# Low-rank maps of an RWKV time mix on two column halves, and their second maps on row halves

## The chip, the cores and the metric

One Trainium2 chip, one of its cores. The metric is the device time of one execution in microseconds (us). A core has five engines that run on their own and meet through semaphores: TensorE (PE in the profile, with its weight loads as PEld), VectorE (DVE), ScalarE (ACT), GpSimd (POOL), and SyncE (SP), which here only issues DMA transfers. ACTq, SPq and so on are the sequencers of the engines, where DMA transfers are issued. Each engine runs its instructions in the order of its own program; a wait holds up everything behind it on that engine.

## The reference

The model is one long chain on 512 tokens of width 1024: a block with an RWKV-7 time mix and a feed-forward, a block with sparse attention and a feed-forward, and a second model's block. Everything is float32. The change touches only the inputs of the time mix (`_rwkv7_time_mix`), which come near the start:

```python
xx = h_prev - h
xs = h[None] + xx[None] * mu[:, None, None, :]
r, k, v = jnp.einsum('pbtd,pde->pbte', xs[:3], w_rkv)
xv, xw, xa, xg = xs[2], xs[3], xs[4], xs[5]
w = -jax.nn.softplus(-(w0 + jnp.tanh(xw @ w1) @ w2)) - 0.5   # decay, w1 is 1024x64, w2 64x1024
a = jax.nn.sigmoid(a0 + (xa @ a1) @ a2)                       # rate,  a1 is 1024x64, a2 64x1024
g = jax.nn.sigmoid(xg @ g1) @ g2                              # gate,  g1 is 1024x160, g2 160x1024
...
kk = kk / jnp.maximum(jnp.sqrt(jnp.sum(kk * kk, -1, keepdims=True)), 1e-12)
decay = jnp.exp(-jnp.exp(heads(w)))
_, y = lax.scan(_rwkv7_step, S0, (tm(rh), tm(decay), tm(kh), tm(vh), tm(-kk), tm(kk * ah)))
```

There are 16 heads of 64. The scan is computed in chunks of 64 tokens, two heads (128 features) at a time.

## The kernel before

Features lie on the 128 partitions, tokens along the free side; the width 1024 is KT = 8 tiles of 128, HD is 64, P is 128. PSUM has eight banks, `ps[:, b, :]`, each 128 partitions by 512 numbers. `mm` (L191) is one float32 product out = left^T right; the profile shows each as two passes on PE, each with its own weight load, so eight matmuls are sixteen rows.

`modulation` (to 36 us) reduces 16 tiles of weights on DVE as they arrive. `time_mix_inputs` follows:

- ACT makes `h` (the profile's branch_in) tile by tile, L299; POOL makes the token shift `xx`, L315; DVE mixes, `mix` L318: for each tile j the three low-rank inputs w, a, g into `tmp` (mixed_low_rank), which has two buffers a kind, so tile j waits for PE's `lora{j-2}`; after the eight tiles it mixes r, k and v, eight tiles each.
- PE, for each tile j, makes four products that accumulate over j: w (64 columns of weights, bank 0, partitions 0 to 63), a (64 columns, bank 1, partitions 0 to 63), g0 (128 columns, bank 2) and g1 (32 columns, bank 3). Before w, a and g0 it waits for the mix that it reads.
- After the last tile ACT reads the four banks: tanh of w, copy of a, sigmoid of g0 and g1 (L302 to L306).
- SP loads the constants of the recurrence (`cr`, const_recurrence) once `lora7` is done; this load brings the semaphore `once_in` to 32.

`recurrence` works on eight pairs of heads. PE first waits for the pair's weights, for ACT's `g1` and for `once_in` at 32. Then come the inputs of pair 0: the projections r into bank 1 and k into bank 0 (eight products each), `decay_and_rate(0)`: the second maps w2 and a2 for this pair, each with 64 rows of contraction, into banks 1 and 0, where ACT has by then read r and k; `kk_sum`, the projection v into bank 4, and `by_tokens`. Then eight turns, one a pair (`turn`). Turn i has five rounds k = 1 to 5, in each a product Y{k}, ACT's copy of it (L585), and from that X{k} and XT{k}. Between these the inputs of pair i+1 are made: r after round 1, k around round 3, `decay_and_rate(i+1)` between Y4 and the wait for ACT's copy of Y4, `kk_sum` after XT4, v around round 5. `each_head` (L433) makes a product for each of the two heads, on partitions 0 to 63 and 64 to 127.

On ACT, `k_input` copies k (L540), waits for DVE's kk0 and squares it (L542); in round 4 it copies Y4, then takes the sigmoid of the decay (L548) and of the rate (L550). The order of all this is written out by hand; nothing plans it.

Elsewhere in the kernel (L1547, L1591) the attention makes two heads' products beside each other: the logits with 64 rows of contraction for each head in a bank of its own, the sums over values with 64 columns for each head on the two partition halves.

Of the kernel before, what the change touches and what calls it, by code (L numbers as in the profile page):

```python
# [8 lines left out]
P = 128  # L9
T = 512  # L10
D = 1024
KT = D // P
# [4 lines left out]
HD = 64  # L17
# [13 lines left out]
ACT = mybir.ActivationFunctionType  # L31
# [70 lines left out]
def build(nc, d):  # L102

    ctx = ExitStack()
    with ctx:
# [33 lines left out]
        ps = ctx.enter_context(nc.psum_tensor("psum", [P, 8, T], F32))  # L139
# [44 lines left out]
        def wtile(s, k, rows=P, width=P, at=0):  # L184
            return slot[s][0:rows, at + k * width:at + (k + 1) * width]
# [5 lines left out]
        def mm(out, lhsT, rhs, start=True, stop=True):  # L191
            return nc.tensor.matmul(out, lhsT, rhs, start=start, stop=stop)  # L192
# [17 lines left out]
        once_in = sem("loaded_once")  # L210
# [62 lines left out]
        MIX = ["r", "k", "v", "w", "a", "g"]  # L273

        def time_mix_inputs(scope, hin, mods_ready):
# [18 lines left out]
            def act(act):  # L294
                act_done.enter(act)
                act.wait_ge(x_in, 16)
                act.wait_ge(*mods_ready)
                for j in range(KT):
                    nc.scalar.activation(h[:, j, :], x[:, j, :], ACT.Identity, bias=mod(0, SH1, j),  # L299
                                                    scale=mod(0, SC1, j)).then_inc(*act_done.step(f"hin{j}"))  # L300
                act.wait_ge(*pe_done(f"lora{KT - 1}"))
                nc.scalar.activation(lora["w"][0:64, :], ps[0:64, 0, :], ACT.Tanh).then_inc(*act_done.step("w"))  # L302
                nc.scalar.activation(lora["a"][0:64, :], ps[0:64, 1, :], ACT.Copy).then_inc(*act_done.step("a"))
                nc.scalar.activation(lora["g0"][:, :], ps[:, 2, :], ACT.Sigmoid).then_inc(*act_done.step("g0"))
                act.wait_ge(zeroed, 1)
                nc.scalar.activation(lora["g1"][0:32, :], ps[0:32, 3, :], ACT.Sigmoid).then_inc(*act_done.step("g1"))  # L306

            def pool(pool):
                pool_done.enter(pool)
# [25 lines left out]
            def pe(pe):  # L335
                pe_done.enter(pe)
                pe.wait_ge(once_in, 16)
                for j in range(KT):
                    w = first[:, j * 288:(j + 1) * 288]
                    for n, (bank, a, b) in enumerate([(0, 0, 64), (1, 64, 128), (2, 128, 256), (3, 256, 288)]):  # L340
                        m = min(n, 2)
                        if n < 3:
                            pe.wait_ge(*dve_done(f"{MIX[3 + m]}{j}"))
                        last = mm(ps[0:b - a, bank, :], w[:, a:b], tmp[:, m, j % 2, :], j == 0, j == KT - 1)
                    last.then_inc(*pe_done.step(f"lora{j}"))

            phase(sp=sp, act=act, pe=pe, dve=dve, pool=pool)
# [13 lines left out]
        def recurrence(scope, h, xs, lora, mix_pe, mix_act, mix_dve):  # L361
# [427 lines left out]
            def pe(pe):  # L789
# [13 lines left out]

                def decay_and_rate(p):
                    pe.wait_ge(*in_act("r", p))
                    mm(ps[:, 1, :], wtile(0, 24, HD), lora["w"][0:HD, :]).then_inc(*in_pe.step("w"))
                    pe.wait_ge(*in_act("k", p))
                    mm(ps[:, 0, :], wtile(0, 25, HD), lora["a"][0:HD, :]).then_inc(*in_pe.step("a"))

                def kk_sum(p):  # L810
                    pe.wait_ge(*in_act("kk sq", p))
# [139 lines left out]
                        last = each_head(bank(4)[:, c, :], yn[:, c, :], eye)  # L951
                    last.then_inc(*pe_done.step("y fm"))
                pe.wait_ge(*loads.arrived(0))
                pe.wait_ge(*mix_act("g1"))
                pe.wait_ge(once_in, 32)
                projection("r", 1, range(KT), True)
                projection("k", 0, range(KT), True)
                decay_and_rate(0)
                kk_sum(0)
                projection("v", 4, range(KT), True)  # L960
                by_tokens(0)
                for i in range(N):
                    turn(i, i < N - 1)
# [1910 lines left out]
```

## Time and profile before

| | us |
|---|---|
| median of 3 runs | 3135.13 (3133.73 to 3135.48) |
| the profiled execution's own time | 3136.09 |
| its span in the trace | 3134.3 |
| PE busy | 2868.2 (92%) |
| PE's weight loads busy | 2086.7 (67%) |
| DVE busy | 1424.7 (45%) |
| ACT busy | 1032.7 (33%) |
| POOL busy | 229.3 (7%) |

The profile has a page (busy times, the span in 40 slices, the chain of work that ended last, the costliest groups) and views of the trace that can be asked for a stretch of time. In the timeline each row has a start, a duration, engine, line, operation, "out<-in", the shape (for PE: rows of contraction * columns of weights, then the moving operand's partitions x elements) and xN, the number of instructions merged in the row; behind it stands how long the engine had been idle and what ended that. Numbers of a merged row are from the first start to the last end. In the windows view PEclk is the clock that PE was granted, 1.00 being 2.4 GHz and 0.50 being 1.2 GHz.

### The profile page before, as it was taken

Reading aid. Unit: us, or ns where it says so; the run is one execution under the profiler, and the core shown is the slowest. Engines: PE = TensorE matmul, PEld = TensorE weight load, DVE = VectorE, ACT = ScalarE, POOL = GpSimd, SP = SyncE. Lnnn points to the kernel's source line nnn. Section 1 sums busy time; section 2 is a strip of 40 time slices with the busy share of each in tenths; the row PEclk is TensorE's granted clock in tenths of the full one; section 3 lists DMA queues with packets and bytes.
Section 4 is the critical chain, followed back from the end, with each engine's and each line's share of the span. In section 5 each row is a group of like instructions: output and inputs, shape, how many; then the busy total and the mean of one; then the engine's idle time right before and its main releaser. Section 6 shows DMA issues by size and latency. Waiting matters only on the chain.

```text
span 3134.3 us, 47831 instructions
## 1 busy us (share of the span) xinstructions
PE 2868.2 (92%) x19030; PEld 2086.7 (67%) x19030; DVE 1424.7 (45%) x2257; ACT 1032.7 (33%) x1526; POOL 229.3 (7%) x220
## 2 busy tenths in 40 slices
PE   4998989888999989998999969999989898899998
PEld 1566666645888844565888848888565565688875
DVE  6466565534333226655333243333234676533335
ACT  1232332204432122544432144431011374344214
POOL 1122232201000010311000000000000100000000
PEclk9999999988999989999999989999869999999999
DMA  5222232232222201112222202322111001222212
GB/s 191 85 99 92 102 119 92 89 114 81 94 94 103 99 31 61 34 41 78 97 94 102 99 27 95 104 98 109 54 69 59 34 2 37 97 95 94 106 63 93
DMA packets 45842, 260.79 MB, mean 83 GB/s; under 512 B 4952, under 2 KB 7400, under 8 KB 26888
## 3 DMA queue, kind: packets, MB, share of 16 engines
q1 hardware_dynamic: 45128, 254.20, 23.2%
q10 hardware_dynamic: 576, 4.57, 0.4%
q8 instruction: 109, 1.79, 0.2%
q14 instruction: 29, 0.24, 0.0%
HBM read 256.59 MB, written 2.15 MB: 83 GB/s over the span
## 4 chain that ended last, share of the span: by engine, by line
PE 84%; DVE 7%; issue 3%; ACT 2%; DMA 2%; POOL 1%; PEld 1%; DVEq 0%; SPq 0%; POOLq 0%; ACTq 0%; PEldq 0%
PE psum L192 82%; PE psum L1572 2%; DMA weights<-in_ada 1%; DVE weights L228 1%; PEld psum L192 1%; DVE ln_rstd L1135 0%; POOL join L508 0%; POOL join L497 0%; POOL XT_pairs L501 0%; DVE rms_rstd L1215 0%; DVE group_norm L766 0%; DVE ff_weights_lo L1247 0%; DVE keys_rstd L2181 0%; DMA embedding<-in_embedding 0%; DVE cmp_blocks L2195 0%
## 5 line engine op out<-in xcount | busy, mean ns | idle before, releaser
L1247 DVE TENSOR_TENSOR ff_weights_lo<-weights,ff_weights_hi 128x1024 fp32r<-128x1024 f32 (+1 forms) x120 | 159.7, 1332 | 330.2 <-ACT ff_weights_hi L1244 330.2
L1247 DVE TENSOR_TENSOR ffn_weights_lo<-weights,ffn_weights_hi 128x1024 fp32r<-128x1024 f32 (+1 forms) x120 | 159.6, 1332 | 322.9 <-ACT ffn_weights_hi L1244 322.9
L192 PE MATMUL psum<-ff_in_hi,ff_weights_hi 128*128 128x512 f32 x704 | 276.3, 393 | 21.0 <-DVE ff_in_lo L1144 17.6
L192 PE MATMUL psum<-ffn_in_hi,ffn_weights_hi 128*128 128x512 f32 x704 | 276.2, 392 | 17.6 <-DVE ffn_in_lo L1223 14.2
L1244 ACT ACTIVATE ffn_weights_hi<-weights 128x1024 fp32r<-128x1024 f32 (+1 forms) x120 | 137.4, 1146 | 448.7 <-PE psum L192 448.7
L1244 ACT ACTIVATE ff_weights_hi<-weights 128x1024 fp32r<-128x1024 f32 (+1 forms) x120 | 137.4, 1146 | 445.6 <-PE psum L192 445.6
L192 PE MATMUL psum<-ff_in_lo,ff_weights_hi 128*128 128x512 f32 x704 | 275.7, 392 | 0.0
L192 PE MATMUL psum<-ffn_in_hi,ffn_weights_lo 128*128 128x512 f32 x704 | 275.6, 391 | 0.0
L192 PE MATMUL psum<-ffn_in_lo,ffn_weights_hi 128*128 128x512 f32 x704 | 275.6, 391 | 0.0
L192 PE MATMUL psum<-ff_in_hi,ff_weights_lo 128*128 128x512 f32 x704 | 275.4, 391 | 0.0
L192 PEld LDWEIGHTS psum<-ff_in_hi,ff_weights_hi 128*128 128x128 f32 x704 | 133.4, 189 | 51.3 <-issue 19.1
L192 PEld LDWEIGHTS psum<-ffn_in_hi,ffn_weights_hi 128*128 128x128 f32 x704 | 133.3, 189 | 48.7 <-issue 16.5
L192 PEld LDWEIGHTS psum<-ff_in_hi,ff_weights_lo 128*128 128x128 f32 x704 | 133.2, 189 | 27.9
L192 PEld LDWEIGHTS psum<-ffn_in_lo,ffn_weights_hi 128*128 128x128 f32 x704 | 133.3, 189 | 27.7
L192 PEld LDWEIGHTS psum<-ff_in_lo,ff_weights_hi 128*128 128x128 f32 x704 | 133.3, 189 | 27.4
L192 PEld LDWEIGHTS psum<-ffn_in_hi,ffn_weights_lo 128*128 128x128 f32 x704 | 133.1, 189 | 27.6
L192 PE MATMUL psum<-ffn_hidden_hi,ffn_weights_hi 128*128 128x512 f32 x352 | 136.9, 389 | 0.0
L192 PE MATMUL psum<-ff_hidden_lo,ff_weights_hi 128*128 128x512 f32 x352 | 136.9, 389 | 0.0
L192 PE MATMUL psum<-ff_hidden_hi,ff_weights_hi 128*128 128x512 f32 x352 | 136.9, 389 | 0.0
L192 PE MATMUL psum<-ff_hidden_hi,ff_weights_lo 128*128 128x512 f32 x352 | 136.9, 389 | 0.0
L192 PE MATMUL psum<-ffn_hidden_lo,ffn_weights_hi 128*128 128x512 f32 x352 | 136.9, 389 | 0.0
L192 PE MATMUL psum<-ffn_hidden_hi,ffn_weights_lo 128*128 128x512 f32 x352 | 136.9, 389 | 0.0
(459 smaller groups left out, 5161.5 us busy)
## 6 DMA issues: line engine op xcount, KB each, us to landing
weights<-in_ada SPq DMA_DIRECT2D x96, 512.0 KB, 4.4
weights<-in_ff_in SPq DMA_DIRECT2D x44, 1024.0 KB, 4.8
weights<-in_ffn_in SPq DMA_DIRECT2D x44, 1024.0 KB, 4.8
weights<-in_ff_out SPq DMA_DIRECT2D x16, 1408.0 KB, 5.9
weights<-in_ffn_out SPq DMA_DIRECT2D x16, 1408.0 KB, 5.9
weights<-in_rwkv SPq DMA_DIRECT2D x8, 1792.0 KB, 8.2
weights<-in_fox_qkv SPq DMA_DIRECT2D x4, 1536.0 KB, 6.7
residual<-in_x ACTq DMA_DIRECT2D x2, 2048.0 KB, 9.7
```

The costliest lines, as they stand in the source:

```text
L192: return nc.tensor.matmul(out, lhsT, rhs, start=start, stop=stop)
L228: return nc.vector.tensor_tensor_reduce(ada_tile(n), ada_tile(n), cond, scale=1.0, scalar=0.0, op0=ALU.mult, op1=ALU.add, accum_out=inner[ ...
L1244: return nc.scalar.activation(sp_.hi[u][:, 0:width], slot[s][:, u * width:(u + 1) * width], ACT.Copy)
L1247: return nc.vector.tensor_tensor(sp_.lo[u][:, 0:width], slot[s][:, u * width:(u + 1) * width], sp_.hi[u][:, 0:width].bitcast(F32), ALU.sub ...
L1572: ins = nc.tensor.transpose(ps[:, TR + hh, blk], probs[:, n % 3, hh, blk], ident)
```

## The change

The weights' columns for w and a now go to two halves of the array: w to partitions 0 to 63 of bank 2, a to partitions 64 to 127 of bank 3, one after the other behind a single wait for the mix of a (which DVE makes after that of w). g0 and g1 go to banks 5 and 6 behind the wait for g. So none of the four uses banks 0, 1 and 4, in which r, k and v are made. ACT writes `lora["a"]` on partitions 64 to 127, and the host puts a2's weights on those partitions (64 rows of zeros ahead). In the recurrence PE's wait for ACT's `g1` moves behind the projections r and k of pair 0, and that for `once_in` at 32 ahead of `by_tokens(0)`, which is PE's first reader of the constants. In `decay_and_rate` both waits (ACT's r and k) stand ahead of both products, and the second one is on rows 64 to 127. The number of products, their sizes, the DMA transfers and the work of DVE, POOL and ACT stay as they are.

```diff
--- before.py
+++ after.py
@@ -299,11 +299,11 @@
                     nc.scalar.activation(h[:, j, :], x[:, j, :], ACT.Identity, bias=mod(0, SH1, j),
                                                     scale=mod(0, SC1, j)).then_inc(*act_done.step(f"hin{j}"))
                 act.wait_ge(*pe_done(f"lora{KT - 1}"))
-                nc.scalar.activation(lora["w"][0:64, :], ps[0:64, 0, :], ACT.Tanh).then_inc(*act_done.step("w"))
-                nc.scalar.activation(lora["a"][0:64, :], ps[0:64, 1, :], ACT.Copy).then_inc(*act_done.step("a"))
-                nc.scalar.activation(lora["g0"][:, :], ps[:, 2, :], ACT.Sigmoid).then_inc(*act_done.step("g0"))
+                nc.scalar.activation(lora["w"][0:64, :], ps[0:64, 2, :], ACT.Tanh).then_inc(*act_done.step("w"))
+                nc.scalar.activation(lora["a"][HD:P, :], ps[HD:P, 3, :], ACT.Copy).then_inc(*act_done.step("a"))
+                nc.scalar.activation(lora["g0"][:, :], ps[:, 5, :], ACT.Sigmoid).then_inc(*act_done.step("g0"))
                 act.wait_ge(zeroed, 1)
-                nc.scalar.activation(lora["g1"][0:32, :], ps[0:32, 3, :], ACT.Sigmoid).then_inc(*act_done.step("g1"))
+                nc.scalar.activation(lora["g1"][0:32, :], ps[0:32, 6, :], ACT.Sigmoid).then_inc(*act_done.step("g1"))
 
             def pool(pool):
                 pool_done.enter(pool)
@@ -337,11 +337,12 @@
                 pe.wait_ge(once_in, 16)
                 for j in range(KT):
                     w = first[:, j * 288:(j + 1) * 288]
-                    for n, (bank, a, b) in enumerate([(0, 0, 64), (1, 64, 128), (2, 128, 256), (3, 256, 288)]):
-                        m = min(n, 2)
-                        if n < 3:
-                            pe.wait_ge(*dve_done(f"{MIX[3 + m]}{j}"))
-                        last = mm(ps[0:b - a, bank, :], w[:, a:b], tmp[:, m, j % 2, :], j == 0, j == KT - 1)
+                    pe.wait_ge(*dve_done(f"a{j}"))
+                    for n in range(2):
+                        mm(ps[n * HD:(n + 1) * HD, 2 + n, :], w[:, n * HD:(n + 1) * HD], tmp[:, n, j % 2, :], j == 0, j == KT - 1)
+                    pe.wait_ge(*dve_done(f"g{j}"))
+                    for bank, a, b in ((5, 128, 256), (6, 256, 288)):
+                        last = mm(ps[0:b - a, bank, :], w[:, a:b], tmp[:, 2, j % 2, :], j == 0, j == KT - 1)
                     last.then_inc(*pe_done.step(f"lora{j}"))
 
             phase(sp=sp, act=act, pe=pe, dve=dve, pool=pool)
@@ -803,9 +804,9 @@
 
                 def decay_and_rate(p):
                     pe.wait_ge(*in_act("r", p))
+                    pe.wait_ge(*in_act("k", p))
                     mm(ps[:, 1, :], wtile(0, 24, HD), lora["w"][0:HD, :]).then_inc(*in_pe.step("w"))
-                    pe.wait_ge(*in_act("k", p))
-                    mm(ps[:, 0, :], wtile(0, 25, HD), lora["a"][0:HD, :]).then_inc(*in_pe.step("a"))
+                    mm(ps[:, 0, :], wtile(0, 25)[HD:P, :], lora["a"][HD:P, :]).then_inc(*in_pe.step("a"))
 
                 def kk_sum(p):
                     pe.wait_ge(*in_act("kk sq", p))
@@ -951,13 +952,13 @@
                         last = each_head(bank(4)[:, c, :], yn[:, c, :], eye)
                     last.then_inc(*pe_done.step("y fm"))
                 pe.wait_ge(*loads.arrived(0))
-                pe.wait_ge(*mix_act("g1"))
-                pe.wait_ge(once_in, 32)
                 projection("r", 1, range(KT), True)
                 projection("k", 0, range(KT), True)
+                pe.wait_ge(*mix_act("g1"))
                 decay_and_rate(0)
                 kk_sum(0)
                 projection("v", 4, range(KT), True)
+                pe.wait_ge(once_in, 32)
                 by_tokens(0)
                 for i in range(N):
                     turn(i, i < N - 1)
@@ -2814,7 +2815,8 @@
     d["ada"] = np.concatenate([a["ada_w"][i].T.reshape(6 * KT, P, D) for i in range(2)])
     d["c_rows"] = np.broadcast_to(a["c"].reshape(1, D), (P, D))
     d["lora1"] = rows(np.concatenate([a["rwkv_w1"][0], a["rwkv_a1"][0], a["rwkv_g1"][0]], 1))[None]
-    second = [tiles(pad(w, P)) for w in (a["rwkv_w2"][0], a["rwkv_a2"][0], a["rwkv_g2"][0][:P], a["rwkv_g2"][0][P:])]
+    second = [tiles(pad(w, P)) for w in (a["rwkv_w2"][0], np.concatenate([np.zeros_like(a["rwkv_a2"][0]), a["rwkv_a2"][0]]),
+                                         a["rwkv_g2"][0][:P], a["rwkv_g2"][0][P:])]
     d["rwkv"] = np.concatenate([tiles(a["rwkv_w_rkv"][0, m]) for m in range(3)] + second, 2)
     d["rwkv_out"] = tiles(a["rwkv_w_out"][0])
```

## Rows read from the trace of the kernel before

**Rows 1.** The page, the chain that ended last, share of the span by engine.

```profile
PE 84%; DVE 7%; issue 3%; ACT 2%; DMA 2%; POOL 1%; PEld 1%; DVEq 0%; SPq 0%; POOLq 0%; ACTq 0%; PEldq 0%
```

**Rows 2.** Timeline, PE and its weight loads, first tile of the low-rank maps.

```profile
39.55 33.57 PE L192 MATMUL psum<-mixed_low_rank,lora_first 128*64 128x512 f32 x64 [39.55 <-DVE mixed_low_rank L318]
40.91 0.18 PEld L192 LDWEIGHTS psum<-mixed_low_rank,lora_first 128*64 128x64 f32 x1 [1.10 <-DVE mixed_low_rank L318]
...
43.13 0.50 PEld L192 LDWEIGHTS psum<-mixed_low_rank,lora_first 128*128 128x128 f32 x2 [1.61 <-DVE mixed_low_rank L318]
44.83 0.14 PEld L192 LDWEIGHTS psum<-mixed_low_rank,lora_first 128*32 128x32 f32 x2 [1.20 <-issue]
45.80 0.19 PEld L192 LDWEIGHTS psum<-mixed_low_rank,lora_first 128*64 128x64 f32 x2 [0.84 <-DVE mixed_low_rank L318]
```

**Rows 3.** Timeline, weight loads of the fifth tile (j = 4).

```profile
57.48 0.19 PEld L192 LDWEIGHTS psum<-mixed_low_rank,lora_first 128*64 128x64 f32 x2 [0.84 <-issue]
...
59.34 0.30 PEld L192 LDWEIGHTS psum<-mixed_low_rank,lora_first 128*128 128x128 f32 x2 [0.81 <-DVE mixed_low_rank L318]
60.40 0.14 PEld L192 LDWEIGHTS psum<-mixed_low_rank,lora_first 128*32 128x32 f32 x2 [0.76 <-issue]
61.37 0.19 PEld L192 LDWEIGHTS psum<-mixed_low_rank,lora_first 128*64 128x64 f32 x2 [0.84 <-issue]
```

**Rows 4.** Timeline, the mixes on DVE, and POOL's token shift.

```profile
37.98 11.42 DVE L318 SCALAR_TENSOR_TENSOR mixed_low_rank<-token_shift,vectors,branch_in 128x512 f32<-128x512 f32 x9 [2.23 <-POOL token_shift L315]
...
36.82 10.71 POOL L315 TENSOR_TENSOR token_shift<-branch_in 128x512 f32<-128x512 f32 x8 [35.42 <-ACT branch_in L299]
...
61.58 2.08 DVE L318 SCALAR_TENSOR_TENSOR mixed_low_rank<-token_shift,vectors,branch_in 128x512 f32<-128x512 f32 x3 [1.81 <-PE psum L192]
...
67.47 5.38 DVE L318 SCALAR_TENSOR_TENSOR mixed_r<-token_shift,vectors,branch_in 128x512 f32<-128x512 f32 x8
```

**Rows 5.** Timeline, from the low-rank maps to decay and rate.

```profile
73.16 0.59 ACT L302 ACTIVATE lora_w<-psum 64x512 f32<-64x512 f32 x1 [31.56 <-PE psum L192]
...
76.03 0.57 ACT L306 ACTIVATE lora_g<-psum 32x512 f32<-32x512 f32 x1
76.90 0.50 PEld L192 LDWEIGHTS psum<-mixed_r,weights 128*128 128x128 f32 x2 [4.69 <-issue]
...
86.39 7.03 PE L192 MATMUL psum<-mixed_k,weights 128*128 128x512 f32 x16
...
93.35 0.29 PEld L192 LDWEIGHTS psum<-lora_w,weights 64*128 64x128 f32 x2 [0.76 <-issue]
```

**Rows 6.** Windows: length, PE, PEld, DVE, ACT, POOL busy, PEclk, DMA share, GB/s.

```profile
70.00:73.20 3.20, 3.12 (x7) 0.57 (x5) 3.20 (x6) 0.04 (x1) 0.00 (x0) 1.00 0.00 0
...
76.90:81.50 4.60, 4.57 (x6) 2.00 (x7) 4.60 (x8) 0.00 (x0) 0.00 (x0) 0.50 0.01 4
```

**Rows 7.** Timeline, attention: two heads on row halves, then on column halves.

```profile
1293.01 1.13 PE L192 MATMUL psum<-dsa_keys,scaled_queries 64*128 64x512 f32 x4
...
1294.87 1.09 PE L192 MATMUL psum<-attention_in,dsa_values 128*64 128x128 f32 x16
...
1295.89 0.30 PEld L192 LDWEIGHTS psum<-dsa_keys,scaled_queries 64*128 64x128 f32 x4 [0.17 <-issue]
```

**Rows 8.** Timeline, round 4 of the first turn.

```profile
145.26 0.60 ACT L540 ACTIVATE k<-psum 128x512 f32<-128x512 f32 x1 [8.74 <-PE psum L192]
...
146.16 1.12 PE L192 MATMUL psum<-lora_w,weights 64*128 64x512 f32 x2
...
147.13 0.58 ACT L585 ACTIVATE b_pairs<-psum 128x512 f32<-128x512 f32 x1
...
148.07 1.15 PE L192 MATMUL psum<-b_pairs,XT_pairs 64*64 64x64 f32 x32
```

**Rows 9.** Timeline, decay and rate of pair 0.

```profile
94.11 0.40 PEld L192 LDWEIGHTS psum<-lora_a,weights 64*128 64x128 f32 x2 [0.46 <-ACT k L540]
...
95.14 0.67 ACT L548 ACTIVATE sig<-psum,pair_vectors 128x512 f32<-128x512 f32 x1
```

## The prediction

> **What bounds the kernel now.** I read the page first. The chain that ended last is 84% PE [rows 1], so PE's program is the clock of this kernel, and the question is how many microseconds PE loses between 39 us, where its first product starts, and 94 us, and once in each turn. Then the timeline of that stretch, PE with its weight loads. The reader should see three things in it. First, from 39.55 to 73.1 us PE works through the 64 passes of the low-rank maps nearly without a break [rows 2, 3]. Second, PE then stands until 76.90, because its next product waits for ACT's last sigmoid, which ends at 76.60 [rows 5]. Third, behind that pause PE runs at half its clock: the granted clock reads 1.00 up to 73.2 and 0.50 from 76.9 to 81.5 [rows 6]. At full clock a pass on 512 columns of tokens takes 0.43 us (16 in 7.03 us, less a tail of about 0.2 [rows 5]); at half it takes 0.85.
>
> **A step of the low-rank maps.** A tile j takes 61.37 - 57.48 = 3.89 us: the four passes of w and a up to 59.34 (1.86), the two of g0 up to 60.40 (1.06), the two of g1 up to 61.37 (0.97) [rows 3]. That is eight passes of 0.427, 3.42 us, and 0.47 for three changes of the array's shape. DVE needs 2.08 us for the three mixes of a tile, and its idle 1.81 us were a wait for PE [rows 4]: PE is the bound here.
>
> With w and a on two column halves, do their passes run side by side? The attention does this already: sixteen passes with 64 columns, in pairs on the two halves, start at 1294.87, and the next shape starts at 1295.89 [rows 7], 1.02 us later. One pass of 128 columns of moving data is a quarter of 0.427, 0.107 us; sixteen in a row would be 1.71, eight slots are 0.85, and with 0.17 for the change of shape that is the measured 1.02. So four passes cost two slots, and I take 1.86 - 0.854 = 1.01 us for w and a. The two bounds are full overlap (0.854 saved a step) and none (0); full overlap is the nearer row, differing only in that its moving data is 128 long and not 512, and in using one bank where the change uses two. The step becomes 3.89 - 0.85 = 3.04 us. DVE stays behind it: 2.08 us of mixes and some 0.2 us of signal for each 3.04.
>
> The Trainium skill speaks against this step: "TensorE: Matmul & The Clock Gate", on packing small matmuls (what overlaps and what doesn't), says that a weight load overlaps a running matmul only where the two use different row groups, and the two column halves share all rows. By that rule the four weight loads of a step would lie open. The attention's sixteen passes in 1.02 us leave no room for it, so the trace doesn't agree, and I keep the rule as a rival only.
>
> **The first step.** PE now waits for the mix of a, not of w: it starts at 40.95 (the weight load of a was let go at 40.91 by DVE [rows 2]) in place of 39.55. Here PE is at the lower clock: g0's two passes take 44.83 - 43.13 = 1.70, g1's 0.97 [rows 2], so full speed came near 44.6, some 5.1 us after PE's start. I assume the same 5.1 us after the new start, 46.05; the bounds are 44.6 again and 48.5. Then w and a take 40.95 to 42.66, g0 42.8 to 44.5, g1 44.65 to 46.2, and tile 1 starts at 46.35, 0.55 later than 45.80. DVE is no hindrance: nine mixes in 11.42 us while POOL makes the token shift until 47.53 [rows 4] put the mix of a for tile 1 at about 45.2, that of g at 46.7 and a for tile 2 at 48.7, each ahead of its reader. Tiles 1 to 7 take 7 x 3.04, so the maps end at 67.6 against 73.1. **Saved: 7 x 0.85 - 0.55 = 5.4 us** (4.5 to 6.0 by the bounds of the clock).
>
> **The pause.** The projections r and k use banks 1 and 0, no longer those of the maps, and PE's waits for `g1` and for the constants stand behind them. What is late next? Weights for pair 0 are long there; the mixes of r start when tile 7 is mixed, by PE's `lora5` at 61.5 + 0.2 + 2.08 = 63.8, and take 0.67 each (eight in 5.38 [rows 4]): the first is ready at 64.5, the last at 69.2, while PE reads one in 0.86 us from 67.7 on; k follows at the same rate. Nothing holds PE. ACT's four reads take 3.4 us from 67.7 [rows 5] and end at 71, far ahead of their first reader at 81. SP's load of the constants goes out at 67.6 and is wanted by DVE only after the mixes of v, near 80. **Saved: 76.90 - 73.04 = 3.9 us.**
>
> **The clock.** r and k take 93.35 - 76.90 = 16.45 us now [rows 5]. PE comes to them at the granted 1.00 [rows 6] and without a pause, so 32 passes at 0.43 are 13.7, with the change of shape 13.8. **Saved: 2.65 us.** The lower end is 0 if the level drops all the same.
>
> **Decay and rate of pair 0.** Both maps now wait for ACT's k: they start where a's did, at 94.11 [rows 9], against 93.35 for w. Four passes in two slots (the four 64-row passes of the attention, rows in halves and banks apart, take 1.13 us in all [rows 7], where four in a row would be 1.71 and a tail) and the usual 0.6 to the result give w at 95.2; the sigmoid that reads it started at 95.14 [rows 9], held up until then by the square. **Lost: 0.1 us** (0 to 0.3).
>
> **Round 4 of seven turns.** PE's w now waits for k as well. ACT's copy of k ends at 145.86 and w starts at 146.16 behind Y4 [rows 8], so the wait is over just before it ends: 0, with 0.1 as the upper bound. Queued behind it are a, X4 and XT4. The four passes end at 147.0 in place of 147.9. Then X4 needs ACT's copy of Y4, which ends at 147.71 [rows 8] and doesn't move, since ACT was held by DVE's kk0 and the square. X4 starts at 147.8 against 148.07: 0.27 of the 0.85 us remains. The other six turns show the same rows with the same gaps (a's start to X4's 0.94 or 0.95). **Saved: 7 x 0.27 = 1.9 us**, between 0 (if the turn's later steps on DVE set its end) and 2.
>
> **Sum.** 5.4 + 3.9 + 2.65 - 0.1 + 1.9 = 13.7 us. Everything behind is tied to PE by semaphores, so it moves as a whole. The profiled execution's 3136.09 (span 3134.3 and 1.8 around it) becomes 3122.4; it lay 1.0 above the median, which becomes 3135.1 - 13.7 = 3121.4, rounded to 3121.5.
>
> **Rivals.**
> *A. The column halves overlap in part or not at all.* Without overlap a step stays 3.89, the first tile ends near 47.1, the maps at 74.3, and the sum is 1.2 lost there, + 3.9 + 2.65 - 0.1 + 1.9 = 7.1: 3128.0. With the four weight loads of 0.14 open in each step it is 13.7 - 8 x 0.55 = 9.3: 3125.8; that is what the page's rule above would make of it. For it: no row has column halves with 512 tokens. Against: rows 7.
> *B. The clock takes part of it back.* Full speed comes a good two microseconds later at the start (1 us), or one more drop like the one behind the pause falls in a turn (2.65 us, the price of the one seen): 3122.4 to 3126. For it: the drop of rows 6 shows what one pause costs, and round 4 now has an 0.8 us pause of PE in each turn; against: that pause is a fifth of the 3.9 us that cost the clock.
> *C. The turns give nothing, or the inputs' gain is partly swallowed* (DVE's reductions that wait for their DMA in the rounds): 3123.4 to 3129.
> *D. Slower.* The paired passes run at the lower clock throughout the maps: two passes side by side count as one slot, PE works fewer passes in a step, and the chip never grants 1.00. Then a step is 6 x 0.854 + 0.47 = 5.6 us, the maps end at 67.6 + 7 x 2.56 = 85.5, r and k take today's 16.45, and decay and rate come at 102.0, 8.7 later than now; less 1.9 in the turns, that is 3141.9. It ends on the slower side only if all seven later tiles and the start of r are slow; with five slow tiles and r and k at full clock the whole is about even. Against it: the attention's paired passes run at full-clock spacing [rows 7].
>
> **Numbers.** Forecast, 3118.5 to 3124.5: 0.62, 3121.5 the likeliest (what lies lower than 3118.5 I leave out). A: 0.15. B beyond that range: 0.10. C beyond it: 0.10. D: 0.03. A rest lower than 3118.5, if turns gain more than I see. The range 3118.5 to 3128 takes in A's both ends. A measurement of this kernel tells some 0.2%, 6.3 us, from no change, so faster means below 3128.8: 0.92; same 0.05; slower 0.03.
>
> **What would show it.** Low-rank weight loads some 3.04 us apart from tile to tile (3.5 to 3.9: A); first load near 40.9, ACT's tanh near 67.7; PE going from the maps to r without idle, r and k in 13.8 us, PEclk 1.00 from 70 to 80 (0.50: D or a drop in spite of no pause); ACT's k near 81.5; X4 in round 4 let go by ACT's copy with a pause of about 0.8 us before it, the turns about 0.27 shorter. The prediction is wrong if a step of the maps is set by something other than PE's slots, if the mixes of r are late for PE, or if the seven turns don't keep what was won ahead of them.

## The result and the profile after

The changed kernel's median is 3117.09 us (3112.11 to 3121.03, 5 runs) against 3134.89 us (3132.10 to 3135.48, 5 runs): a ratio of 0.9944, interval 0.9930 to 0.9959. It is faster by 17.8 us, 0.56%. Forecast were 3121.5 us and a range of 3118.5 to 3128: the sign was right, the gain was 4 us larger than the sum, and the time lies 1.4 us below the range. Over all timings of this study, these ten among them, 65 of the kernel before have a median of 3133.6 (3126.8 to 3140.0, standard deviation 2.8) and 16 of the changed kernel 3117.9 (3112.1 to 3121.3, 2.4): 15.7 us between them. The pool holds chips that differ a little; where both kernels were timed on one chip again, the medians were 16.4 (e4) and 16.9 us (e13) apart. The three timings of before that the prediction saw were much closer together than that (3133.7 to 3135.5).

The profiled execution took 3118.73 us with a span of 3116.9. The page's chain is still PE's (answers to [rows 1]):

```profile
PE 84%; DVE 6%; issue 3%; ACT 3%; DMA 2%; POOL 1%; PEld 1%; DVEq 0%; SPq 0%; POOLq 0%; ACTq 0%; PEldq 0%
```

Timeline of the changed kernel, weight loads of the first tile and of a later one (answers to [rows 2, 3]); DVE's first mix starts at 38.84 here, 37.98 before:

```profile
41.83 0.33 PEld L192 LDWEIGHTS psum<-mixed_low_rank,lora_first 128*64 128x64 f32 x4 [41.83 <-issue]
...
43.76 0.50 PEld L192 LDWEIGHTS psum<-mixed_low_rank,lora_first 128*128 128x128 f32 x2 [1.61 <-DVE mixed_low_rank L318]
45.76 0.18 PEld L192 LDWEIGHTS psum<-mixed_low_rank,lora_first 128*32 128x32 f32 x2 [1.50 <-issue]
46.91 0.20 PEld L192 LDWEIGHTS psum<-mixed_low_rank,lora_first 128*64 128x64 f32 x4 [0.96 <-DVE mixed_low_rank L318]
...
59.07 0.20 PEld L192 LDWEIGHTS psum<-mixed_low_rank,lora_first 128*64 128x64 f32 x4 [0.84 <-DVE mixed_low_rank L318]
...
60.08 0.30 PEld L192 LDWEIGHTS psum<-mixed_low_rank,lora_first 128*128 128x128 f32 x2 [0.81 <-DVE mixed_low_rank L318]
61.13 0.14 PEld L192 LDWEIGHTS psum<-mixed_low_rank,lora_first 128*32 128x32 f32 x2 [0.76 <-issue]
62.11 0.20 PEld L192 LDWEIGHTS psum<-mixed_low_rank,lora_first 128*64 128x64 f32 x4 [0.84 <-DVE mixed_low_rank L318]
```

Four weight loads of w and a now stand in one row of 0.20 us, and g0 follows 1.01 us behind them in place of 1.86; the tile takes 62.11 - 59.07 = 3.04 us. Then the seam to r, and ACT's k (answers to [rows 5]):

```profile
68.19 0.30 PEld L192 LDWEIGHTS psum<-mixed_r,weights 128*128 128x128 f32 x2 [0.84 <-issue]
...
68.30 0.59 ACT L302 ACTIVATE lora_w<-psum 64x512 f32<-64x512 f32 x1 [25.84 <-PE psum L192]
...
71.32 0.57 ACT L306 ACTIVATE lora_g<-psum 32x512 f32<-32x512 f32 x1
...
82.23 0.60 ACT L541 ACTIVATE k<-psum 128x512 f32<-128x512 f32 x1 [6.21 <-PE psum L192]
```

PE's loads for r come 0.11 us before ACT's tanh, no pause is left. Round 4 of the first turn (answers to [rows 8]):

```profile
136.74 0.69 PE L192 MATMUL psum<-lora_w,weights 64*128 64x512 f32 x1
136.75 0.69 PE L192 MATMUL psum<-lora_a,weights 64*128 64x512 f32 x1
...
137.71 0.58 ACT L586 ACTIVATE b_pairs<-psum 128x512 f32<-128x512 f32 x1
...
138.34 1.15 PE L192 MATMUL psum<-b_pairs,XT_pairs 64*64 64x64 f32 x32 [0.47 <-ACT b_pairs L586]
```

w and a start 0.01 us apart, and X4 follows 1.60 us behind w in place of 1.91; it waits for ACT's copy, as foretold, with PE idle for 0.47 us and not some 0.8.

What the sum did not have is in the timeline ahead of pair 0's by_tokens, where PE stands for 2.58 us, and in the windows view of the same kernel (columns as in [rows 6]):

```profile
95.47 1.15 PE L192 MATMUL psum<-const_recurrence,b_pairs 64*64 64x64 f32 x32 [2.58 <-issue]
```

```profile
95.00:97.00 2.00, 1.15 (x32) 1.04 (x32) 0.92 (x1) 0.34 (x1) 2.00 (x2) 1.00 0.00 0
97.00:101.00 4.00, 3.90 (x35) 2.67 (x36) 0.94 (x3) 1.54 (x2) 1.26 (x2) 0.57 0.00 0
...
171.00:179.00 8.00, 4.02 (x124) 3.64 (x120) 5.28 (x8) 1.52 (x4) 5.88 (x6) 1.00 0.56 219
179.00:183.00 4.00, 3.50 (x71) 3.54 (x73) 0.00 (x0) 0.99 (x2) 2.49 (x2) 0.57 0.01 4
```

The granted clock falls to its lower level (1.2 GHz) for a few microseconds behind stretches in which PE stood about half the time. The kernel before has such drops too. The table gives the stages from timeline starts, as means over four profiles of each kernel (the first, and those of the experiments), with the smallest and the largest. v_tok is ACT's copy of a pair's v by tokens, the first thing that ACT does in a turn, so it marks where each turn begins; the last group norm is taken at DVE's sum (L765 in the changed kernel).

| stage, us | before | changed | difference | sum's term |
|---|---|---|---|---|
| DVE's first mix to ACT's tanh (the maps) | 34.73 (34.39 to 35.18) | 29.30 (29.16 to 29.46) | -5.4 | -5.4 |
| tanh to r's first weight load | 3.75 (3.70 to 3.85) | -0.11 | -3.9 | -3.9 |
| from there to ACT's k | 15.94 (15.73 to 16.56) | 14.04 (14.03 to 14.04) | -1.9 | -2.65 |
| ACT's k to the first v_tok | 20.03 (19.70 to 20.43) | 21.82 (21.44 to 22.87) | +1.8 | +0.1 |
| first to eighth v_tok: seven turns | 488.84 (487.61 to 490.01) | 486.34 (485.81 to 487.65) | -2.5 | -1.9 |
| eighth v_tok to the last group norm | 43.9 (41.3 to 45.5) | 43.7 (41.3 to 45.1) | -0.2 | 0 |
| all that follows | 2485.1 (2483.8 to 2486.7) | 2482.5 (2480.1 to 2485.9) | -2.6 | 0 |

The spans' means are 3130.5 and 3116.4, 14.1 apart, since the first mix also starts 0.6 later in the changed kernel's profiles, in a stage of DMA and DVE that the change doesn't touch.

### The profile page after: what moved, and what is told of

It is laid out like the page before. It is cut to its first block, busy times and chain, and to the rows that moved or that the text cites. A ratio compares the mean times of both kernels' runs of the same rounds, so it can differ in the third digit from the quotient of the medians.

```text
span 3116.9 us, 47838 instructions
## 1 busy us (share of the span) xinstructions
PE 2841.3 (91%) x19030; PEld 2069.7 (66%) x19030; DVE 1425.2 (46%) x2257; ACT 1033.2 (33%) x1526; POOL 229.9 (7%) x220
## 4 chain that ended last, share of the span: by engine, by line
PE 84%; DVE 6%; issue 3%; ACT 3%; DMA 2%; POOL 1%; PEld 1%; DVEq 0%; SPq 0%; POOLq 0%; ACTq 0%; PEldq 0%
PE psum L192 82%; PE psum L1573 2%; DMA weights<-in_ada 1%; DVE weights L228 1%; PEld psum L192 1%; DVE ln_rstd L1136 0%; POOL join L509 0%; POOL join L498 0%; POOL XT_pairs L502 0%; DVE rms_rstd L1216 0%; DVE group_norm L767 0%; DVE ff_weights_lo L1248 0%; DVE keys_rstd L2182 0%; DVE cmp_blocks L2196 0%; ACT nsa_probs L1609 0%
```

## The experiments

The theory: the sum is right stage by stage, and what goes beyond it are drops of the clock, at the places that the granted clock shows and whose number varies from execution to execution (theory 1). Its rival: one part of the change is worth more than its term, above all the row halves, by what they set off later in a turn (theory 2).

**Column halves alone (e1).** The kernel before with

```diff
-for n, (bank, a, b) in enumerate([(0, 0, 64), (1, 64, 128), (2, 128, 256), (3, 256, 288)]):
+pe.wait_ge(*dve_done(f"a{j}"))
+for n in range(2):
+    mm(ps[n * HD:(n + 1) * HD, n, :], w[:, n * HD:(n + 1) * HD], tmp[:, n, j % 2, :], j == 0, j == KT - 1)
+pe.wait_ge(*dve_done(f"g{j}"))
+for bank, a, b in ((2, 128, 256), (3, 256, 288)):
...
-mm(ps[:, 1, :], wtile(0, 24, HD), lora["w"][0:HD, :])
+mm(ps[:, 1, :], wtile(0, 24), lora["w"][:, :])
```

(and the same for a, with zeros on the unused rows).

> The kernel before with the column halves and the single wait of a tile alone: w in bank 0, a on partitions 64 to 127 of bank 1, g0 and g1 in banks 2 and 3, PE's waits for g1 and the constants ahead of r, the second maps one after the other on all 128 rows (zeros below or above, made once by GpSimd at the start). By my sum: tiles 3.04 us apart, the maps end some 5.4 us earlier, the pause of 3.9 us and the slow start of r stay, turns as before: 5.4 us less than before. If the column halves had given more than the sum said, tiles would be closer than 3.04. Whatever else moves the time is then a change in the clock drops of the turns, a few us either way.

Measured: 3128.17 against 3134.40 on the same chip, ratio 0.9980 (0.9970 to 0.9990), 6.2 us less. Its timeline, weight loads of a tile, then the seam:

```profile
59.12 0.20 PEld L192 LDWEIGHTS psum<-mixed_low_rank,lora_first 128*64 128x64 f32 x4 [0.84 <-DVE mixed_low_rank L320]
...
62.16 0.20 PEld L192 LDWEIGHTS psum<-mixed_low_rank,lora_first 128*64 128x64 f32 x4 [0.84 <-DVE mixed_low_rank L320]
...
68.36 0.59 ACT L303 ACTIVATE lora_w<-psum 64x512 f32<-64x512 f32 x1 [25.64 <-PE psum L192]
...
72.10 0.30 PEld L192 LDWEIGHTS psum<-mixed_r,weights 128*128 128x128 f32 x2 [4.69 <-issue]
```

The step is 3.04 us, the pause of 3.74 us stays. The maps take 29.26 us against 34.73, the mean of before: the term of 5.4 is confirmed by itself.

**Own banks and moved waits alone (e2).**

```diff
-[(0, 0, 64), (1, 64, 128), (2, 128, 256), (3, 256, 288)]
+[(2, 0, 64), (3, 64, 128), (5, 128, 256), (6, 256, 288)]
...
-pe.wait_ge(*mix_act("g1"))
-pe.wait_ge(once_in, 32)
 projection("r", 1, range(KT), True)
 projection("k", 0, range(KT), True)
+pe.wait_ge(*mix_act("g1"))
```

> The kernel before with own banks (2, 3, 5, 6) and the moved waits alone. By my sum the tiles stay 3.89 us apart, r follows the maps at once and at full clock: from the maps' end to ACT's k 14.0 us in place of 20.3, so 6.5 us less than before. If the clock drops of the turns are a lottery by execution, the whole may differ from that by some 3 us either way, and the distance from ACT's first k to the end of the recurrence differs from that of before only where PEclk is below 1.

Measured: 3127.58 against 3134.40, ratio 0.9979 (0.9970 to 0.9988), 6.8 us less. The timeline:

```profile
72.04 0.14 PEld L192 LDWEIGHTS psum<-mixed_low_rank,lora_first 128*32 128x32 f32 x2 [0.76 <-issue]
73.01 0.30 PEld L192 LDWEIGHTS psum<-mixed_r,weights 128*128 128x128 f32 x2 [0.84 <-issue]
...
73.12 0.59 ACT L302 ACTIVATE lora_w<-psum 64x512 f32<-64x512 f32 x1 [30.69 <-PE psum L192]
...
87.05 0.60 ACT L540 ACTIVATE k<-psum 128x512 f32<-128x512 f32 x1 [6.22 <-PE psum L192]
```

From r's load to k it is 14.04 us. A part of what that gains was lost behind it: k to the first v_tok took 21.15 us, 1.4 more than in the first profile of before, with PEclk below 1.00 from about 101.5.

**The change without row halves (e3).** The changed kernel with the four lines of `decay_and_rate` as

```diff
+mm(ps[:, 1, :], wtile(0, 24), lora["w"][:, :])
 pe.wait_ge(*in_act("k", p))
-mm(ps[:, 1, :], wtile(0, 24, HD), lora["w"][0:HD, :])
-mm(ps[:, 0, :], wtile(0, 25)[HD:P, :], lora["a"][HD:P, :])
+mm(ps[:, 0, :], wtile(0, 25), lora["a"][:, :])
```

> The changed kernel with the second maps of decay and rate as before: one after the other, the wait for k between them, on all 128 rows (zeros in the other half, made once by GpSimd). Theory 1 (the sum was right, what exceeds it is the clock): 1.9 us slower than the changed kernel in the median of many, 0.27 in each turn's round 4, drops in the turns as many as in both. Theory 2 (row halves are worth more in a turn than 0.27, by what they trigger later): 4 to 6 us slower than the changed kernel, near 3121.5, with each undisturbed turn 0.6 us longer.

Measured: 3120.28, ratio 0.9957 (0.9945 to 0.9969), against 3117.97 for the changed kernel on the same chip: 2.3 us slower, with overlapping intervals, so the times alone don't tell 1.9 from 4. The seven turns are 66.5, 69.7, 72.5, 69.6, 71.0, 69.4, 69.8. The undisturbed ones (69.4 to 69.6) are some 0.3 us longer than the changed kernel's 69.2 and not 0.6, which is theory 1's size; the turn of 72.5 us is taken up below.

**The changed kernel again (e4).** No edit.

> The changed kernel once more. Theory 1: its times scatter over several us again (3112 to 3121 so far), and the profile shows the drops of PEclk in the turns at other places and of other number than the first profile; every stage at full clock has the same length to 0.1 us. Theory 2: the lengths of the turns are those of the first profile: 67.4, 70.6, 69.2, 70.7, 69.2, 70.7, 68.0.

Measured: 3117.97 (3115.36 to 3118.53), ratio 0.9946 (0.9933 to 0.9959). The turns are 68.9, 69.2, 70.7, 69.2, 70.7, 69.2, 68.0 against 67.4, 70.6, 69.2, 70.7, 69.2, 70.7, 68.0 in the first profile: other turns carry the drop, each costing 1.5 us, the lengths of the others agree to 0.1 us.

**Row halves alone (e10).** The kernel before with the changed `decay_and_rate`, the host's shifted weights, and

```diff
-nc.scalar.activation(lora["a"][0:64, :], ps[0:64, 1, :], ACT.Copy)
+nc.scalar.activation(lora["a"][HD:P, :], ps[0:64, 1, :], ACT.Copy)
```

> The kernel before with the second maps on row halves and the merged wait alone (ACT writes the map of a to partitions 64 to 127 from partitions 0 to 63). By my sum: 7 x 0.27 - 0.1 = 1.8 us less than before, undisturbed turns 69.17 in place of 69.45 to 69.56. If the row halves also keep the long drops away (turns over 72 us, one in each profile of a kernel without them and none in three with them), 4 us less than before and no such turn.

Measured: 3129.13 against 3131.19 on that chip, ratio 0.9990 (0.9981 to 0.9999): 2.1 us less, of the sum's size, though the interval goes from 0.3 to 6 us. No turn is longer than 70.7 us. The timeline of PE in round 4, and turns of 69.2 us where the clock doesn't drop:

```profile
147.65 0.69 PE L192 MATMUL psum<-lora_w,weights 64*128 64x512 f32 x1
147.65 0.69 PE L192 MATMUL psum<-lora_a,weights 64*128 64x512 f32 x1
...
149.25 0.97 PE L192 MATMUL psum<-b_pairs,XT_pairs 64*64 64x64 f32 x25 [0.47 <-ACT b_pairs L585]
```

This kernel keeps the pause ahead of r (3.71 us behind the tanh), and yet its r and k take 14.04 us and run at the full clock from the first pass:

```profile
77.64 0.30 PEld L192 LDWEIGHTS psum<-mixed_r,weights 128*128 128x128 f32 x2 [4.66 <-issue]
78.18 0.19 PEld L192 LDWEIGHTS psum<-mixed_r,weights 128*128 128x128 f32 x1 [0.24 <-issue]
```

So the pause doesn't always bring the clock down: of seven profiles with it (four of before, e1, e5 and e10), six show the slow start and this one doesn't.

The parts alone give 6.2 (e1), 6.8 (e2) and 2.1 us (e10), 15.1 together, where the sum had 5.4, 6.5 and 1.8.

**Unread products in PE's waits, both kernels (e5, e6).** A helper makes products of constants into bank 7, which nobody reads:

```diff
+def fill(n):
+    each_head(ps[:, 7, 0:n], eye, cr[:, 0:n])
```

with two of 512 columns ahead of by_tokens(0) and of Nak (the third of the four products that open a turn, behind which X0 and the rounds come), one ahead of y fm (the output back by features), 256 or 512 ahead of the waits for the chunks' states S4 to S6, 384 in the rounds of the last turn.

> The kernel before with products that nobody reads (into bank 7, from constants) where PE waits in the recurrence: two of 0.85 us ahead of the inputs' by_tokens(0) and of Nak, one ahead of y fm, 0.4 to 0.85 us before the waits for the states S4 to S6, 0.64 us in each round of the last turn. If PE's waits at the turn's end bring the clock down and the drops cost time: PEclk 1.00 from 95 us to the end of the recurrence except for the slow start of r, every turn of the same length, 68.5 to 69.6 us, 3 to 8 us less than before in all, with less scatter. If the drops cost nothing: no gain, or a loss of the products' own time that the waits don't hide, 0.5 us a turn.

> The changed kernel with the same unread products. If the clock's drops are what my sum lacked, this against the kernel before with the same products is the sum's own difference, 13.7 us (12 to 15), its turns are 0.27 to 0.4 shorter than those, and it is 2 to 5 us faster than the changed kernel. If instead row halves or moved waits gave more than the sum said by another way, the difference stays 17 us with the clock level in both.

Measured: before with them 3130.82, ratio 0.9992 (0.9983 to 1.0001), so no gain that can be told; changed with them 3120.63, ratio 0.9961 (0.9947 to 0.9975), 2.7 us above the changed kernel's pooled 3117.9 and not 2 to 5 below. The two are 10.2 us apart, less than the 12 to 15 expected. The profiles show that three drops at the heads of turns stayed in either kernel. The changed kernel with the products has turns of 70.7 and 70.8 us where its first profile had 70.6 and 70.7, and shows, in the windows view,

```profile
173.00:178.00 5.00, 3.23 (x96) 2.98 (x96) 2.55 (x4) 0.19 (x1) 3.80 (x4) 1.00 0.40 152
178.00:182.00 4.00, 3.50 (x67) 3.53 (x69) 0.00 (x0) 1.00 (x2) 2.49 (x3) 0.57 0.00 0
```

a stretch behind Nak in which PE waits for GpSimd twice (1.4 and 0.7 us), and which had no product in it. The drop ahead of the first turn did go: k to the first v_tok takes 19.92 us. Why the pair is no further apart is not shown; the spans of its profiles differ by 11.7 us. What the pair does give is the row halves' price at the full clock: undisturbed turns of 69.17 against 69.45, 0.28 a turn, 1.96 in seven, the sum's 1.9.

**Unread products where the drops are (e9).** The changed kernel with products only in by_tokens(0) and ahead of Nak as above, and

```diff
+fill(512)
 pe.wait_ge(*pool_done("XT0", i))
...
+if k == 1:
+    fill(384)
 pe.wait_ge(*pool_done(f"A{k}", i))
```

> The changed kernel with unread products only where its profiles show the drops: in by_tokens(0) of pair 0 (2 x 0.85 us into a wait of 2.6), ahead of Nak (2 x 0.85 into 2.3), ahead of X0 (0.85 into 1.0 to 1.4) and ahead of the first round (0.64 into 0.74). If the drops of the turns' first ten microseconds come from PE's half busy stretch there: PEclk 1.00 from 95 us to the last turn, all turns 69.2 long (in place of 69.2 and 70.7 by turns), 5 to 7 us faster than the changed kernel, near 3112. If the drops fall for another reason, turns of 70.7 remain, and the products cost what of them isn't hidden.

Measured: 3113.15 against 3131.19 on its chip, ratio 0.9943 (0.9930 to 0.9957). The turns are 68.8, 69.2, 69.2, 69.2, 69.3, 69.1, 68.0, and k to the first v_tok takes 19.91 us in place of 21.5. Its PE timeline and windows:

```profile
241.30 1.89 PE L192 MATMUL psum<-const_recurrence 64*64 64x512 f32 x8
243.78 1.15 PE L192 MATMUL psum<-a_pairs,k_pairs 64*64 64x64 f32 x32 [0.59 <-ACT g L581]
...
245.67 1.06 PE L192 MATMUL psum<-const_recurrence 64*64 64x512 f32 x4
247.25 1.15 PE L192 MATMUL psum<-const_recurrence,XT_pairs 64*64 64x64 f32 x32 [0.53 <-POOL XT_pairs L502]
```

```profile
95.00:170.00 75.00, 70.28 (x1206) 47.86 (x1206) 40.93 (x65) 21.85 (x32) 18.11 (x14) 1.00 0.31 104
...
240.00:310.00 70.00, 65.35 (x1144) 44.67 (x1140) 41.99 (x68) 22.43 (x33) 18.00 (x14) 1.00 0.33 114
```

That a drop in the turn's first ten microseconds costs 1.5 us and comes from PE's half idle stretch there is shown: with the stretch filled it is gone, and with it the turns of 70.7 (and so again in e14). Three drops remain in the seven turns, at places where PE isn't the last (near 231, 439 and 507), and cost 0.2 us at most. The products have a price in the first turn: 68.8 us, against 67.4 in the changed kernel where it has no drop there, since PE has no wait ahead of that turn's Nak. Against the kernel before on its own chip, though, the gain is 18.0 us, no more than the changed kernel's, so the total did not show the 5 to 7 us expected; the two kernels run side by side in e13 and e14.

**A wait of its own for w (e11).** The changed kernel with

```diff
-pe.wait_ge(*dve_done(f"a{j}"))
 for n in range(2):
+    pe.wait_ge(*dve_done(f"{MIX[3 + n]}{j}"))
```

> The changed kernel with a wait of its own for w ahead of w's product. In the first tile PE then starts 1.45 us earlier, as before; the pairs stay whole from tile 1 on, as both mixes are there. By my sum the first tile ends some 0.5 us earlier and nothing else moves: from DVE's first mix to ACT's first k 42.9 in place of 43.4 us.

Measured: 43.09 us from the first mix to ACT's k, against 43.22 (43.09 to 43.39) in four profiles of the changed kernel. The first tile does start earlier:

```profile
40.26 0.29 PEld L192 LDWEIGHTS psum<-mixed_low_rank,lora_first 128*64 128x64 f32 x2 [40.26 <-issue]
...
45.40 0.19 PEld L192 LDWEIGHTS psum<-mixed_low_rank,lora_first 128*64 128x64 f32 x2 [0.84 <-issue]
45.98 0.19 PEld L192 LDWEIGHTS psum<-mixed_low_rank,lora_first 128*64 128x64 f32 x2 [0.40 <-DVE mixed_low_rank L318]
47.43 0.30 PEld L192 LDWEIGHTS psum<-mixed_low_rank,lora_first 128*128 128x128 f32 x2 [1.25 <-DVE mixed_low_rank L318]
```

but in tile 1 PE waits for DVE's slow mixes, twice, and most of the 1.4 us is given back. The single wait costs 0.1 us, not 0.5, and even that can't be told from none, since 43.09 also stands among the changed kernel's four. This profile has no drop ahead of the first turn: k to the first v_tok takes 19.91 us.

**Without row halves again (e12).** No edit against e3.

> The changed kernel without row halves once more, for its profile. If a turn over 72 us belongs to the serial second maps, one of the seven is again of 72.5 us; if it is luck, it is absent in one profile or another. Undisturbed turns 69.45 to 69.56, those with one drop 70.98.

Measured: turns of 66.5, 72.7, 69.5, 71.0, 69.4, 71.0, 68.3: a long one again. k to the first v_tok takes 19.71 us, without a drop there, though PE comes to r without a pause.

**What was still open: the slow start, the long turns, and the products side by side (e13 to e16).** e15 and e16 are the kernel before, e13 is the changed kernel, e14 has the edits of e9 and e11 together.

> The kernel before, third profile, for the slow start of r and the turns. If the 2.65 us by which the sum priced the slow start was a long drop of one profile, r and k take 14.7 to 15 us here in place of 16.45; if it was typical, 16.45. A turn over 72 us if that belongs to the serial second maps.

> The kernel before, fourth profile, with the same two questions: r and k 14.7 to 15 or 16.45 us, and whether one of the seven turns is over 72 us. If both kernels' stages behind the recurrence differ as much from profile to profile of one kernel as between the kernels (2391 to 2397 us so far), nothing of the change's effect lies there.

Measured: from r's load to ACT's k 15.74 us in both (15.73 in the second profile of before, 16.56 only in the first). Timeline of the third profile, r's weight loads:

```profile
77.16 0.30 PEld L192 LDWEIGHTS psum<-mixed_r,weights 128*128 128x128 f32 x2 [4.80 <-issue]
...
78.67 0.33 PEld L192 LDWEIGHTS psum<-mixed_r,weights 128*128 128x128 f32 x1 [0.35 <-DVE mixed_k L318]
79.53 0.33 PEld L192 LDWEIGHTS psum<-mixed_r,weights 128*128 128x128 f32 x1 [0.52 <-issue]
...
81.97 0.19 PEld L192 LDWEIGHTS psum<-mixed_r,weights 128*128 128x128 f32 x1 [0.40 <-DVE mixed_v L318]
```

Four passes or so stand 0.85 us apart here, against six in the first profile. The turns are 67.7, 69.5, 71.0, 69.4, 71.0, 69.4, 69.6 and 67.7, 69.5, 71.0, 69.4, 70.9, 69.6, 71.4: none over 72 us. So the kernel before doesn't have one in every profile. What a long turn is, the granted clock shows. The windows view of before's first profile, its turn of 72.6 us:

```profile
320.00:324.40 4.40, 2.25 (x77) 2.14 (x75) 4.03 (x7) 1.26 (x3) 2.65 (x3) 0.99 0.97 404
324.40:334.60 10.20, 8.49 (x156) 8.14 (x153) 1.07 (x3) 1.79 (x3) 5.49 (x5) 0.50 0.14 55
```

The low stretch lasts 10.2 us there, and the turn costs 3 us; in the turns of 70.7 and 71.0 it lasts 3.4 us, for 1.5. The seventh turn of 71.4 us in e16 (and of 71.3 in the first profile) has the same 10.2 us; without a drop it takes 68.0 to 68.3. Counted this way, seven of eight profiles with serial second maps and unfilled turns have a stretch of 10.2 us in a turn, and none of six with row halves; why, no run shows.

> The changed kernel beside the next one on the same chip. If the drops explain what the sum lacked, its difference to the kernel before comes out at 13.7 to 17 again, and its seven turns add up to 485.8 to 487.6, at least 1 us below any profile with serial second maps (488.3 to 490.0).

> The changed kernel with the unread products of e9 and a wait of its own for w. If the drops in the turns are worth what the turns' lengths say (three of 1.5 us, and 1.5 to 3 in the inputs of pair 0), it is 4 to 6 us faster than the changed kernel on the same chip. If the clock gives elsewhere what it takes here, the two are within 2 us.

Measured (e13 and e14 on one chip): before 3134.81, changed 3117.87 (ratio 0.9952, 0.9938 to 0.9965), with the products and the wait for w 3109.74 (3108.21 to 3117.26; 0.9928, 0.9914 to 0.9941): 8.1 us below the changed kernel, more than the 4 to 6 expected, and 25 below the kernel before. It has the lowest median of this study, though the two intervals just overlap. In the profiles its seven turns take 482.88 us against 487.65, and k to the first v_tok 19.92 against 21.47, 6.3 us in the stages that the products touch, while their spans differ by 0.6 only (3115.5 and 3116.1), because what follows the recurrence took 2484.9 and 2480.1. The profiled execution with the products was the slowest of its five (3117.26). The seven turns of the changed kernel came to 487.65 here, not at least 1 us below every profile with serial maps (487.61 in e15): that part of the expectation fell.

**Both kernels in one more profile (e7, e8).** No edits.

> The kernel before once more, for its profile. If the drops in the turns are a lottery by execution, other turns than the fourth and the seventh carry the long ones (the first profile: 67.6, 69.7, 69.6, 72.6, 69.6, 69.6, 71.3), and the sum of the seven turns is another by up to 3 us. If they follow from the kernel's own times, the list is the same.

> The changed kernel once more, for its profile: seven turns that add up to 485.8 and 485.9 in the first two. If the kernel has a course of its own that keeps it clear of the long drops, no turn is over 71 us again; if it was luck, one of 72.5 us shows up here, as in each profile without row halves.

Measured: before 3129.32 with turns of 67.7, 69.7, 69.6, 72.6, 69.6, 71.0, 68.3; changed 3118.07 with 67.4, 69.2, 70.7, 69.2, 70.7, 69.2, 69.6. In before the first five turns are those of the first profile and only the last two differ, so the drops are no pure lottery; the changed kernel has no turn over 71 us again. Windows of the changed kernel's third profile, round 1 of the third turn:

```profile
247.00:250.00 3.00, 1.21 (x34) 1.01 (x32) 0.69 (x1) 0.36 (x1) 2.69 (x3) 1.00 0.01 5
250.00:254.00 4.00, 3.67 (x72) 3.70 (x74) 0.00 (x0) 0.83 (x2) 2.34 (x2) 0.57 0.02 4
```

## Why the prediction was right in its steps and wrong in its number

**The step of the maps** was right: 3.04 us a tile, 5.4 saved, both in the whole and alone (e1). Full overlap on column halves holds with 512 columns of moving data too, and the four weight loads of a pair take 0.20 us, the last of them under running passes. Rival A is out. The rule of the Trainium skill's page "TensorE: Matmul & The Clock Gate", on packing small matmuls, that a weight load overlaps a running matmul only where the row groups differ, doesn't describe these rows: the two column halves share all rows.

**The first tile** was mis-sized in a small way: tile 1 starts 8.07 us after DVE's first mix against 7.82 before, 0.25 later and not 0.55; the full clock came earlier than assumed (g1 took 1.15 us there, not 1.55). From tile 1 on the maps ran at the full clock, so rival D is out as well.

**The pause** was right: 3.9 us in the whole and in e2, and nothing else was late behind it.

**The clock behind the pause** was over-sized: 2.65 us in the sum, 1.9 as a mean of four profiles, 1.7 in three of them. The one profile that the prediction had, happened to hold the longest slow start. At the full clock r and k took 14.04 us to ACT's k every time. And e10 had the same pause and no slow start at all.

**Decay and rate of pair 0.** The 0.1 us itself was 0.2: without a drop the stage takes 19.91 us with the merged wait (e11, and filled in e6, e9 and e14) and 19.70 or 19.71 without it (the first profile of before, e5, e7, e12). What the sum lacked is the drop behind it: the granted clock falls near 97 in all four profiles of the changed kernel, after PE has stood ahead of by_tokens(0), and the stage became 1.8 us longer. The drop isn't the change's alone (before has it in e15 and e16, near 105), nor sure with it (e11 and e12 have none), and PE stands as long there in before's first profile (2.52 us against 2.58), which has no drop. In e15 and e16 it costs less, 20.4 and 20.3 us in place of 21.4 to 22.9.

**Round 4** was right in mechanism and size: X4 let go by ACT's copy, 0.31 us saved in the first turn, 0.28 in every undisturbed turn. Row halves alone gave 2.1 us of the whole, leaving them out cost 2.3, against the sum's 1.9. The seven turns are 2.5 us shorter in the mean; the 0.6 beyond are drops.

**The sum** then is -5.4 - 3.9 - 1.9 + 1.8 - 2.5 = -11.9 us in the stages that the change touches, against the forecast's -13.7. The four profiles of each kernel show -14.1 in all, with 2.6 us from stages behind the recurrence, in which not one instruction differs and whose length goes from 2480 to 2487 us over all profiles.

**The step that failed** is the one under the sum, that everything behind is tied to PE and so "moves as a whole". Every drop of the clock but the one behind the pause was put at nothing that way. By the trace's records of the granted clock, 65 us of the first 670 of the profile that the prediction read were at the lower level, in eleven stretches, and only one of them was in the sum. The first profiles of the two kernels, whose spans are 17.4 us apart, show what stood in its place. The seven turns gave 4.2 us and not 1.9, with 10.2 us at the lower clock against 37.5; the last turn gave 2.0 and all that follows 1.7, where the sum had nothing; 1.8 were lost ahead of the first turn. The mechanism is rival B's, the clock, but in balance it gave where rival B had it take.

The stages behind the recurrence go with the clock too. Over all 18 profiles they had 209 to 226 us at the lower clock, and their length follows it (correlation 0.89, some 0.43 us for each us at the lower clock). The four profiles of before had 220.7 us in the mean, the four of the changed kernel 215.9, which makes 2.1 of the 2.6 us. That the changed kernel has fewer or shorter drops is measured; whether for a reason or by luck of four profiles stays open.

**The range** failed for a second reason: the scatter of the kernel was read from three timings 1.75 us apart. It is 2.8 us in standard deviation, 13 us from end to end. A median of five such timings against another is uncertain by several microseconds by itself, and the range reached 3 us below the forecast. The chances add up to 1.00 without the rest lower than 3118.5, which the prediction named and gave nothing, and there the result fell. Of the 4 us by which the first comparison exceeded the forecast, 1 to 2 vanish with more timings (15.7 pooled, 16.4 and 16.9 on one chip).

## What to carry to other kernels

Two maps of 64 columns each that read different data cost as much as one, if they go to different partition halves and their waits are merged; look in the trace for another place where the kernel already does it, and take the price from there. Where a pause of PE is removed, count what it did to the clock separately and from more than one profile, and look for the next stretch in which PE stands half the time, since the clock may fall there as well. Before giving a range, count the drops in the whole profile: three close timings say little of a kernel that has eleven.

## What the runs showed of the hardware that was not expected

- In the inputs of pair 0 and the turns the granted clock fell although PE never stood for longer than 2.6 us at a time; ahead of the fall at 179 it was busy for 4.02 of 8 us (171 to 179). In e10, on the other hand, PE stood for 3.7 us between the maps and r and the clock did not fall.
- To 650 us the low stretches lasted 3.4 to 13.7 us. One of 3.4 us at the head of a turn costs 1.5 us, one of 10.2 us costs 3, and one near the states' products, where PE waits for DVE, 0.2 at most (e9).
- Products that nobody reads, put into PE's waits, take the drops at the head of a turn away if they lie in the right waits (e9 and e14, the five middle turns take 69.1 to 69.4), and leave them if not (e6, turns of 70.7 and 70.8).
- Two products on the two row halves start 0.01 us apart (136.74 and 136.75), four weight loads on the two column halves take 0.20 us together, where two of the same shape take 0.19 [rows 3].
